# PEER rows in another order: lane dots from PSUM, tile 1's sums of the phase before on TensorE

## The reference

```python
q = (xb @ w_q).reshape(PEER_BLOCK, PEER_HEADS, 2, PEER_HALF)
s = jnp.einsum('thpd,hpnd->thpn', q, sub_keys)
sv, si = lax.top_k(s, PEER_TOPK)
...
experts = jnp.take_along_axis(cidx, fi, axis=-1)
g = jax.nn.softmax(fs, axis=-1).astype(xb.dtype)
hid = jax.nn.gelu(jnp.einsum('td,thkd->thk', xb, u[experts]))
return jnp.einsum('thk,thkd->td', g * hid, v[experts])
```

## Time and profile before

| | |
|---|---|
| median of 3 runs | 3921.12 us (3905.39 to 3923.93) |
| the profiled execution, its own time | 3898.55 us |
| its span, first to last instruction | 3896.7 us |
| granted TensorE clock, mean | 0.807 |
| PE / DVE / ACT / POOL busy | 62% / 75% / 14% / 62% |
| bytes moved by DMA | 1295.78 MB, of which 1073.87 MB expert rows |

### The profile page before, as it was taken

How to read it: one execution, slowest core, us unless ns; L and a number is a source line. 1 busy time by engine, 2 the same in 40 slices (tenths; PEclk the granted TensorE clock), 3 DMA queues, 4 the chain that set the end, 5 groups by cost and what they waited for, 6 DMA issues and landing times. The chain is left out here.

```text
span 3896.7 us, 29311 instructions
## 1 busy us (share of the span) xinstructions
PE 2408.7 (62%) x8928; PEld 1667.8 (43%) x8928; DVE 2923.2 (75%) x5647; ACT 531.2 (14%) x1237; POOL 2397.6 (62%) x2052
## 2 busy tenths in 40 slices
PE   8899527786798617767598717687788815600000
PEld 6676412464585313345486413355576513200000
DVE  2311786788877896778888797788777797798889
ACT  2310001122211101112110101122210101100000
POOL 0000377776675677766676577776566577777775
PEclk9989769997798859888698958998799968955555
DMA  4234699999899889999899989999799988999998
GB/s 176 96 107 140 213 324 361 369 392 348 294 408 409 339 316 347 368 384 392 325 389 409 352 321 347 361 390 391 291 365 409 370 323 308 355 350 367 368 387 339
DMA packets 359900, 1295.78 MB, mean 333 GB/s; under 512 B 40512, under 2 KB 40768, under 8 KB 359744
## 3 DMA queue, kind: packets, MB, share of 16 engines
q0 software_dynamic: 294912, 1073.87, 72.9%
q1 hardware_dynamic: 64256, 217.94, 14.8%
q10 hardware_dynamic: 576, 2.10, 0.1%
HBM read 1291.65 MB, written 2.10 MB: 332 GB/s over the span
## 5 line engine op out<-in xcount | busy, mean ns | idle before, releaser
L1057 POOL DMA_INDIRECT ring<-in_peer_u,eidx x1024 | 1222.6, 1194 | 960.1 <-DVE eidx L1181 475.1
L1057 POOL DMA_INDIRECT ring<-in_peer_v,eidx x1024 | 1174.8, 1147 | 516.8 <-issue 288.1
L1094 DVE CUSTOM_DVE_ANT_0 ring<-ring,hp 128x1024 f32<-128x1024 f32 x1024 | 1236.4, 1224 | 266.0 <-DMA ring<-in_peer_u,eidx 254.1
L1099 DVE SCALAR_TENSOR_TENSOR acc<-ring,wgt,acc 128x1024 f32<-128x1024 f32 x744 | 949.2, 1290 | 123.4 <-DMA ring<-in_peer_v,eidx 101.2
L519 PE MATMUL bank<-xt,panel 128*128 128x256 f32 x4096 | 952.8, 392 | 33.7 <-ACT raw L854 8.5
L519 PEld LDWEIGHTS bank<-xt,panel 128*128 128x128 f32 x4096 | 804.1, 198 | 164.0 <-issue 27.0
L752 PE MATMUL bank<-ring,dg 128*128 128x512 f32 x1120 | 549.6, 632 | 497.2 <-ACT dg L826 363.7
L752 PEld LDWEIGHTS bank<-ring,dg 128*128 128x128 f32 x1120 | 208.9, 198 | 825.4 <-issue 578.6
L594 PE MATMUL bank<-dg,ex 128*128 128x128 f32 x640 | 112.8, 349 | 149.2 <-DVE dg L1341 84.5
L594 PEld LDWEIGHTS bank<-dg,ex 128*128 128x128 f32 x640 | 105.4, 257 | 161.3 <-issue 145.7
L715 PE MATMUL bank<-yt,panel 128*128 128x256 f32 x768 | 173.6, 379 | 0.0
(11 more groups left out here) (164 smaller groups left out, 1884.0 us busy)
## 6 DMA issues: line engine op xcount, KB each, us to landing
panel<-in_panels SPq DMA_DIRECT2D x368, 512.0 KB
ring<-in_peer_u,eidx POOLq DMA_INDIRECT x1024
ring<-in_peer_v,eidx POOLq DMA_INDIRECT x1024
work<-in_rel_bias SPq DMA_DIRECT2D x16, 512.0 KB
gb<-in_ln_g SPq DMA_DIRECT2D x8, 512.0 KB
gb<-in_ln_b SPq DMA_DIRECT2D x8, 512.0 KB
panel<-in_keys SPq DMA_DIRECT2D x16, 256.0 KB
work<-in_x SPq DMA_DIRECT2D x4, 512.0 KB, 5.2
```

Source lines behind the costliest of these rows:

```text
L1057: pool.indirect_dma_start(ring[:, n % RING, :], None, t_in["peer_u" if kind == "U" else "peer_v"], bass.IndirectOffsetOnAxis(ap=eidx[:, t, ...
L1094: v.tensor_tensor_reduce(row, row, hp[:, t, :], 1.0, 0.0, ALU.mult, ALU.add, hid[:, t, c:c + 1]).then_inc(used, 1)
L1099: stt(out=acc[:, t, :], in0=row, scalar=wgt[:, t, c:c + 1], in1=acc[:, t, :], op0=ALU.mult, op1=ALU.add).then_inc(used, 1)
```

## The change

- The order now runs over all phases at once, and a row carries its phase p. In lanes 1 to 3 of a phase come U rows (phase 0: 40, 56, 56, heads in order, both tiles; later phases: 32 each, all of tile 0, lane `it` taking heads 2(it-1) and 2(it-1)+1), merged with V rows of tile 1 of the *preceding* phase that were kept back (26, 26, 12 in phase 1; 40, 40, 16 in phases 2 and 3; in lane 3 they stand beside the first 16 U rows only). Behind the lanes come the first 96 V rows of tile 0 (in phase 0 merged with 32 of tile 1) merged with the U rows that are left, then 64 V rows of both tiles alternating, and what is left of tile 1's V rows goes to the next phase's lanes (in phase 3: to the end of the tail, 96 rows).
- The numbers of rows per stage change as LANE_ROWS and MIXER_ROWS say; what is left for the tail is 416 rows.
- PE sums all V rows of tile 1 in stage T, DVE those of tile 0; one sum group per phase, in banks 6 and 7. Its addition into acc and `finish` of the phase before move from behind lane 0 (and behind lane 3) to call 7 of lane 3.
- ACT copies tile 0 of hp into banks 4 and 5 before the lanes (`hp_near`), and both tiles into banks 4 to 7 before G (`hp_gate`). Dots of U rows of tile 0 in stage T, and all dots in G and O, read these copies.
- GELU and weights are made per head and tile. `eidx` is kept for two phases. PE waits later, ahead of the first scores of A, for the lanes' use of the banks.

```diff
+U_LANES = [(0, 40, 56, 56)] + [(0, 32, 32, 32)] * (PHASES - 1)
+V_LANES = [(0, 0, 0, 0), (0, 26, 26, 12)] + [(0, 40, 40, 16)] * (PHASES - 2)
+NORM_AT = 7
+
+
+def merged(a, b):
+
+    order = sorted([((2 * i + 1) * len(b), 0, i) for i in range(len(a))]
+                   + [((2 * i + 1) * len(a), 1, i) for i in range(len(b))])
+    return [(a, b)[j][i] for _, j, i in order]
...
+    def of(p, kind, t, heads):
+        return [(p, kind, head, k, t) for head in heads for k in range(TOP)]
+
+    rows, back = [], []
+    for p in range(PHASES):
+        n = sum(U_LANES[p])
+        if p:
+            u = of(p, "U", 0, range(HEADS)) + of(p, "U", 1, range(HEADS))
+        else:
+            u = [r for head in range(HEADS) for t in range(TILES) for r in of(p, "U", t, [head])]
+        lanes, u = u[:n], u[n:]
+        for it in range(1, LANES):
+            mine, lanes = lanes[:U_LANES[p][it]], lanes[U_LANES[p][it]:]
+            v, back = back[:V_LANES[p][it]], back[V_LANES[p][it]:]
+            beside = len(mine) // 2 if it == LANES - 1 and v else len(mine)
+            rows += merged(v, mine[:beside]) + mine[beside:]
+        assert not back
+        v0, v1 = of(p, "V", 0, range(HEADS)), of(p, "V", 1, range(HEADS))
+        after = sum(V_LANES[p + 1]) if p + 1 < PHASES else 0
+        early = len(v1) - LAST // 2 - after if p + 1 < PHASES else 0
+        first = merged(v0[:len(v0) - LAST // 2], v1[:early])
+        rows += merged(first, u) + merged(v0[len(v0) - LAST // 2:], v1[early:early + LAST // 2])
+        back = v1[early + LAST // 2:]
+    rows += back
...
-LANE_ROWS = (0, 40, 64, 64)
-MIXER_ROWS = {"A": (16, 60), "B": (8, 32), "C": (12, 56), "G": (16, 64), "O": 16}
+LANE_ROWS = [[u + v for u, v in zip(U_LANES[s], V_LANES[s])] for s in range(PHASES)]
+MIXER_ROWS = [None, {"A": (12, 48), "B": (8, 28), "C": (8, 44), "G": (8, 60), "O": 16}] + [
+    {"A": (12, 52), "B": (8, 32), "C": (12, 48), "G": (12, 64), "O": 16}] * (PHASES - 2)
...
+            plan += [((s, "T", it, i), k) for i, k in enumerate(spread(LANE_ROWS[s][it], CHOICES))]
+    left = PHASES * ROWS - sum(k for _, k in plan)
...
-    kind, head, k, t = STREAM[n % ROWS]
-    s, stage, it, i = KEY_OF[n]
-    return kind == "V" and stage == "T" and (it > 1 or it == 0 and k % 2 == 1)
+    p, kind, head, k, t = STREAM[n]
+    return kind == "V" and t == 1 and KEY_OF[n][1] == "T"
+
+
+def is_near(n):
+
+    p, kind, head, k, t = STREAM[n]
+    return kind == "U" and t == 0 and KEY_OF[n][1] == "T"
 
...
+        bank = [wide[i // 2][:, i % 2 * 512:i % 2 * 512 + 512] for i in range(8)]
+        hp_near = wide[2]
+        hp_gate = wide[2:4]
...
-        pa = bank[4:8]
+        pa = bank[6:8]
...
                 project_qk("A", s, 1)
+                if s:
+                    pe.wait_ge(scores_read, s * LANES)
+                    pe.wait_ge(used, LAST_NEAR[s - 1] + 1)
+                if s > 1:
+                    pe.wait_ge(added, s - 1)
...
+                    group = SUM_ROWS[key[0]]
                     if n == group[0]:
-                        pe.wait_ge(added, sum_group(n))
+                        pe.wait_ge(yc_ev, (key[0] + 1) * 2)
...
-                    if kind == "U" and k == TOP - 1 and t == TILES - 1:
-                        cols = slice(head * TOP, (head + 1) * TOP)
+                    if kind == "U" and k == TOP - 1:
                         act.wait_ge(used, DVE_PLACE[n] + 1)
-                        fn(ge[:, :, cols], hid[:, :, cols], ACT.Gelu_apprx_tanh).then_inc(gelu_done, 1)
+                        fn(ge[:, t, cols], hid[:, t, cols], ACT.Gelu_apprx_tanh).then_inc(gelu_done, 1)
...
             def stage_g(s):
+                if s:
+                    act.wait_ge(e_done["C"], (s + 1) * UNITS * 4)
+                    act.wait_ge(pt_ev["C"], fills_before(s, "C", UNITS))
+                    act.wait_ge(yc_ev, (s + 1) * 2)
+                    for t in range(TILES):
+                        copy(hp_gate[t][:, :], hp[:, t, :]).then_inc(hp_gate_shown, 1)
...
                 take_turned(xt, bank[0:2], h_turned, h_taken, s * 4)
+                act.wait_ge(ln1_done, (s + 1) * TILES)
+                act.wait_ge(e_done["C"], (s + 1) * UNITS * 4)
+                copy(hp_near[:, :], hp[:, 0, :]).then_inc(hp_shown, 1)
                 queries(s, 0)
...
+                        if s and it == LANES - 1 and i == NORM_AT:
+                            finish(s - 1)
...
+                if kind == "U" and k == 0:
                     pool.wait_ge(peer_idx, s * LANES + head // 2 + 1)
...
-                                        bass.IndirectOffsetOnAxis(ap=eidx[:, t, c:c + 1], axis=0)
+                                        bass.IndirectOffsetOnAxis(ap=eidx[:, s % 2, t, c:c + 1], axis=0)
...
-                        v.tensor_tensor_reduce(row, row, hp[:, t, :], 1.0, 0.0, ALU.mult, ALU.add, hid[:, t, c:c + 1]
+                        near = hp[:, t, :]
+                        if is_near(n):
+                            near = hp_near[:, :]
+                            if DVE_PLACE[n] == min(DVE_PLACE[m] for m in rows_of(key) if is_near(m)):
+                                dve.wait_ge(hp_shown, p + 1)
+                        if key[1] in "GO":
+                            dve.wait_ge(hp_gate_shown, key[0] * TILES)
+                            near = hp_gate[t][:, :]
+                        v.tensor_tensor_reduce(row, row, near, 1.0, 0.0, ALU.mult, ALU.add, hid[:, t, c:c + 1]
...
+            def add_sums(s):
+
+                dve.wait_ge(pe_used, PE_PLACE[SUM_ROWS[s][-1]] + 1)
+                dve.wait_ge(used, max(last_sum.values()) + 1)
+                for half in range(2):
+                    part = acc[:, 1, half * 512:(half + 1) * 512]
+                    ins = tt(part, part, pa[half][:, :], ALU.add)
                 ins.then_inc(added, 1)
-                dve.wait_ge(added, group + 1)
+                dve.wait_ge(added, s)
...
+                    i = next(calls)
+                    rows((s, "T", it, i))
+                    if s and it == LANES - 1 and i == NORM_AT:
+                        add_sums(s)
+                        finish(s - 1)
```

More of the change, by code:

```diff
@@ L84 @@
 CHOICES = 10
-def stream():
[L89 to L100, removed]
+U_LANES = [(0, 40, 56, 56)] + [(0, 32, 32, 32)] * (PHASES - 1)
[5 more added lines that the diff above has]
+    return [(a, b)[j][i] for _, j, i in order]
+def stream():
+    def of(p, kind, t, heads):
[21 more added lines that the diff above has]
+    rows += back
+    assert len(rows) == PHASES * ROWS
     return rows
@@ L122, in row_plan @@
             for stage in "AC":
-                before, total = MIXER_ROWS[stage]
+                before, total = MIXER_ROWS[s][stage]
                 if stage == "C":
-                    early, later = MIXER_ROWS["B"]
+                    early, later = MIXER_ROWS[s]["B"]
                     for j, n in enumerate(spread(later, 2)):
@@ L130, in row_plan @@
                     plan += [((s, stage, u, i), k) for i, k in enumerate(spread(n, 5))]
-            before, total = MIXER_ROWS["G"]
+            before, total = MIXER_ROWS[s]["G"]
             plan.append(((s, "G", -1, 0), before))
             plan += [((s, "G", x, 0), k) for x, k in enumerate(spread(total, 12))]
-            plan.append(((s, "O", 0, 0), MIXER_ROWS["O"]))
+            plan.append(((s, "O", 0, 0), MIXER_ROWS[s]["O"]))
             plan.append(((s, "L", 0, 0), LAST // 4))
@@ L163 @@
 DVE_PLACE = {n: i for i, n in enumerate(n for n in range(PHASES * ROWS) if n not in PE_PLACE)}
[L166 to L174, removed]
+SUM_ROWS = {s: [n for n in PE_SUMS if KEY_OF[n][0] == s] for s in range(1, PHASES)}
+LAST_NEAR = {s: max(DVE_PLACE[n] for n in DVE_PLACE if is_near(n) and KEY_OF[n][0] == s) for s in range(PHASES)}
+GELU_NO, WGT_NO = {}, {}
+for _p, _kind, _head, _k, _t in STREAM:
+    if _kind == "U" and _k == TOP - 1:
+        GELU_NO[(_p, _head, _t)] = len(GELU_NO)
+    if _kind == "V" and _k == 0:
+        WGT_NO[(_p, _head, _t)] = len(WGT_NO)
+for _s in range(1, PHASES):
+    assert SUM_ROWS[_s][-1] < RANGE[(_s, "T", LANES - 1, NORM_AT)][1]
 def rows_of(key):
@@ L303, in trunk @@
         iotab = sb("iotab", [P, TOP], BF16)
-        bank = [ctx.enter_context(nc.psum_tensor(f"bank{i}", [P, 512], F32)) for i in range(8)]
+        wide = [ctx.enter_context(nc.psum_tensor(f"wide{i}", [P, D], F32)) for i in range(4)]
+        bank = [wide[i // 2][:, i % 2 * 512:i % 2 * 512 + 512] for i in range(8)]
+        hp_near = wide[2]
+        hp_gate = wide[2:4]
         sc = bank[2:6]
         tp = bank[6:8]
-        pa = bank[4:8]
+        pa = bank[6:8]
         consts_in = sem("consts_in")
@@ L751, in sums @@
                     for half in range(2):
-                        ins = mm(pa[t * 2 + half][:, :], dg[:, i % DIAGS, :], ring[:, n % RING, half * 512:(half + 1) * 512],
+                        ins = mm(pa[half][:, :], dg[:, i % DIAGS, :], ring[:, n % RING, half * 512:(half + 1) * 512],
```

(8 more changed lines are left out.)

49 lines of the change are left out of this document (13 added, 36 removed).

## The result

The changed kernel took **4077.63 us** in the median of 4 runs (4066.09 to 4080.89), against 3920.51 (3905.39 to 3923.93) before: a ratio of **1.042 [1.0394, 1.0446]**, slower. The forecast was 3982 us with a range up to 4038. The granted clock of the profiled execution (0.806 against 0.807) and the bytes (1295.83 MB against 1295.78) hardly changed.

A forecast was written before the change was run, and what follows sets the result against it. No engine was taken as full: the limit changes by stage (PE in the gate stage, POOL's row floor and stalls in lanes). Stage terms summed to +61 us on 3898.6, 3982 us against the median; range 3808 to 4038.

The forecast's parts named there:

- Lanes of phases 2 and 3: Lanes of phases 2 and 3: row floors, index waits, ring holds and lane 3 make 305.9 us against 284, +22 each.
- the held ring: Lanes 1 and 2: the ring held while PE runs the next lane's queries, 9.7 us each, 19.4 together.
- Phase 1's lanes: Lanes of phase 1, with 160 rows: 271.1 us against 287, -16.
- Tail: Stage after the last lanes: 416 rows at 1.40 us plus 22, 605 us against 493, +112.
- Mixers: Stages A to C: each row removed saves 1.0 us, so -36 in phase 1, -18 each in phases 2 and 3.
- G free: Gate stage: PE sets its length, so rows there cost nothing and losing them gains 0.
- Phase 0, -7: Lanes of phase 0: 152 rows, all dots on DVE, 273 us against 280, -7.
- Index waits of 13 us at some twelve places: POOL idle 13.0 us for indices at the start of lanes 2 and 3, ahead of A and of the tail.
- the lane 3 term: Lane 3, phases 2 and 3: DVE needs 81.6 us where POOL needs 59.6 for 48 rows, adding 22.0.
- A PSUM input frees the fetch: Lanes of phases 1 to 3: dots reading PSUM don't hold POOL, removing nearly all the stall, about 50 us each.
- The rival that it frees nothing: Lanes: dots also write to the ring, so stalls stay, +150 us more, 4132 us; chance 0.04.
- Faster rival: Lanes: the stall was the whole limit and backlog covers index waits, sum -113, 3808 us; chance 0.27.

The follow-up runs named there:

- first pair: The changed kernel and the kernel before as first measured, chip not known: 4077.63 us against 3920.51, ratio 1.042.
- before2: The kernel before, unchanged, profiled again on chip 11: 3866.13 us in the median.
- half rows: The kernel before, fetching 512 of 1024 columns of each expert row and using them twice, chip 10: 3880.4 us.
- d_gate: The kernel before with only the dots of gate and output stage reading PSUM copies, chip 4: ratio 1.0039.
- Rows first: The changed kernel with up to 12 V rows at the head of each lane: 1.0057 on chip 10, 1.030 on chip 8, against the kernel before.
- after2: The changed kernel, unchanged, profiled again on chip 11: 3924.62 us, ratio 1.0172 to the kernel before.
- a_sbuf: The changed kernel with all dots reading hp from SBUF again, copies kept, chip 10: 3967.54 us, 1.0287 against the kernel before.
- after3: The changed kernel, unchanged, profiled a third time, chip 8: 4063.23 us, ratio 1.040 to the kernel before.
- c_half_after3: The changed kernel fetching only half of each expert row and using it twice, chip 6: 4077.97 us.
- a_sbuf2: The changed kernel with all dots reading hp from SBUF again, copies kept, chip 8: 4043.73 us, 1.0363 against the kernel before.
- before3: The kernel before, unchanged, profiled again on chip 8: 3905.01 us in the median.

## Why the prediction was wrong

Its direction held, and so did most of its terms where engines start in time; one kind of loss was not in it.

- **Step that failed: "Lanes of phases 2 and 3 ... +22 each", built from POOL's floors and waits alone.** Measured +59 and +58, and +62 on chip 8. On chip 11, where the engines start in time, it is +27.7 and +25.9. There the working fits: lanes 1 and 2 of phase 2 come to 112.1 us each by its terms (72 x 1.242 + 13.0 + 9.7) and took 112.5 and 111.3, lane 3 at 81.6 and took 87.1. The sum assumed that nothing but POOL's queue, the held ring and DVE's work bounds a lane, and put late starts at nothing. They stand in its place: in the changed kernel's lanes of phase 2 the three rows shown hold 46 us of them on VectorE (some would have been waits anyway), ScalarE and TensorE have theirs, and the stage takes 32 us more than on chip 11. Phase 1's lanes likewise: -16 predicted, +17 and +12.6 with late starts, -9.7 with hardly any. That these go together is shown; no run switched late starts on or off by itself, so the 32 us are put down to them and not proven, and what causes them is open. The hint was in the profile of before: 36 us of idle time on DVE put down to issue, and 243 us on ScalarE.
- **Tail, "1.40 us per row", +112.** +136 in the first pair, +113.4 and +108.6 in the others. The row price differs by execution of the same code: (580 - 22)/416 = 1.34, (618 - 22)/416 = 1.43, (628 - 22)/416 = 1.46, and the kernel before moves too (466, 493 and 510 us). The late starts have no part in this: there are 0 to 3 of them in any of these tails. POOL's pace sets the row: the mean fetch in the tail and 0.30 us of issue make 1.34, 1.44 and 1.46 in the changed kernel, and 1.325 in before2 against 1.33 measured, 1.52 against 1.52 with half rows. So the term was right in form, and its size moves with the mean length of a fetch, 481.29 us of POOL in the first pair against 433.12 on chip 11.
- **Mixers, -36, -18, -18**: -37, -19, -13. A row in A to C is worth about 1 us, as taken. **G free**: 115 us, and d_gate shows no gain. **Phase 0, -7**: -15. The sum's +61 is close to chip 11's +68 partly by luck: phase 0 and the mixers of phase 1 gave 14 us more than forecast, lanes and tail took 17 more.
- **Index waits of 13 us at some twelve places**: of POOL's 643.8 us behind L1230, 436.0 is the first wait; the other twelve hold 208 us. The nine at the heads of lanes are 11 to 15 us each, as priced. The three ahead of A and of the tail are 32 to 34 and not 13: POOL is through with lane 3's 48 rows long before DVE, which the lane 3 term itself says (59.6 against 81.6). Rows first takes off 124 us of this wait against after2 and gains 1.1% of time between chips 10 and 11, 0.9% on chip 8.
- **A PSUM input frees the fetch.** The rival that it frees nothing is dead: 0.943 us a fetch with it, 1.08 without in the same order. It is worth 11, 13 and 16 us in the lanes of phases 1 to 3 (a_sbuf on chip 10 against after2 on chip 11), half of the 80 us that a_sbuf's expectation named and some 1.1% in all. On chip 8 no gain in time shows. The Trainium skill, SBUF — State Buffer, Who interferes with whom, infers that two SBUF inputs of such an operation don't hold the descriptors; a_sbuf, which changes that operand alone, disagrees again.
- **Faster rival** (the stall was the whole limit): it wanted the wait for indices covered. DVE's wait for U rows in the lanes of phase 2 is 79.6 us, far over the 15 that would have decided for it. Rows first comes closest, and reaches 1.006.

## What to carry over

Before moving work into a new order, list what each in-order queue will find at its head: here waits of 11 to 15 us at nine places cost about what the PSUM operands won, 1.1% each. And price a row where it leaves and where it goes: on chip 11 the mixers gave back 77 us for 96 rows, while the tail grew by 113 us for its 72. Measure a pair on more than one chip where it can be had: the same two kernels gave 1.017 on two chips and 1.040 to 1.042 on two other occasions, with a narrow interval where there was one. Idle time "issue" is a term of its own, and it has to be looked up for every engine, not only for the busiest.

## What the runs showed of the hardware

**Late starts.** On chips 6, 8 and in the first pair VectorE begins instructions 0.4 to 2 us late, in the changed kernel often in bursts of about ten, with a free engine and nothing awaited. ScalarE has late starts in the same executions, and TensorE more than elsewhere: ScalarE 73 to 129 of them, and none at all in any execution on chips 4, 10 and 11. In the changed kernel bursts begin at the same places: at VectorE's busy instructions 3132, 3318 and 3496 in its first profile, 3133, 3317 and 3498 in after3 and 3134, 3321 and 3500 in c_half_after3, some 180 apart. But a_sbuf2, with the same number of VectorE instructions, has no burst of more than three there, so the place alone doesn't bring one. They don't depend on bytes. The page of after3 has a queue that would fit:

```profile
q8 instruction: 74, 1.21, 0.1%
```

The page of after2 has it too, with 73 packets. 1.21 MB in 74 packets are 16.4 kB each: an engine that reaches a block of its program before it has arrived would look like this. The Trainium skill, Runtime: NRT & Kernel Launch, Instruction fetch mechanics, says that engines refill by blocks of 16 KiB, 256 instructions, and that this is mostly hidden. The packets agree; the bursts would be where it isn't hidden. But the 180 busy instructions between bursts are about 220 with all that the trace records, not 256, and no run changed the number of instructions. So this is argued, not shown. Why some chips show it and others don't, and why VectorE has five times as many in the changed kernel while ScalarE has about the same, stays open.

**The mean fetch moves between executions of the same code.** The tail's code is the same in before2, before3 and d_gate. In before2 336 fetches take 344.30 us; in before3 (chip 8, late starts) and d_gate (chip 4, none in the tail) they take longer:

```profile
3416.00:3926.00 510.00, 0.00 (x0) 0.00 (x0) 439.30 (x518) 4.26 (x9) 384.26 (x337) 0.50 0.94 349
3398.00:3895.00 497.00, 0.00 (x0) 0.00 (x0) 442.88 (x518) 4.26 (x9) 375.18 (x335) 0.50 0.96 358
```

So a slow tail and late starts, which before3's expectation took for one thing, come apart. DVE's busy time is the same (439 to 444 us). That the hold depends on when fetch and operation meet would fit, but no run shows it.
